# Odd mixer of a transformer kernel: products with V moved behind the next weight tile, ropes in two parts, output projection begun early

## The reference, cut to what matters

```python
DL_HEADS = 16; DL_HEAD_DIM = 64
DL_PAIRS = ((128, 1), (512, 4), (2048, 16))

def odd_mixer(x, w_in, w_out, cos, sin):
    B, S, D = x.shape
    q, k, v = jnp.split(x @ w_in, 3, axis=-1)
    ...
    q = partial_rope(heads(q), cos, sin) * (DL_HEAD_DIM ** -0.5)
    k = partial_rope(heads(k), cos, sin)
    v = heads(v)
    outs, lses = [], []
    for (w, d) in DL_PAIRS:
        o, lse = dilated_branch(q, k, v, d, w // d)
        ...
    wts = jax.nn.softmax(jnp.stack(lses, axis=0), axis=0)
    o = jnp.einsum('gbhs,gbhsd->bhsd', wts.astype(v.dtype), jnp.stack(outs, axis=0))
    return o.transpose(0, 2, 1, 3).reshape(B, S, D) @ w_out

mix = odd_mixer(x, od_w_in[j], od_w_out[j], cos, sin)
x = layer_norm(ALPHA * x + mix, ln1_g[l], ln1_b[l])
```

## Time and profile before

| | |
|---|---|
| median of 3 runs | 3791.18 us (3788.5 to 3801.71) |
| the profiled execution, its own time | 3791.59 us |
| its span | 3789.8 us |
| TensorE busy | 3436.3 us, 91% |
| VectorE busy | 2059.0 us, 54% |
| ScalarE busy | 1491.5 us, 39% |
| odd mixer, first attention step to the projection's start | 3052 to 3298 us |
| projection | 3298 to 3342 us |

### The profile page before, as it was taken

How to read it: one execution, slowest core, us unless ns; L and a number is a source line. 1 busy time by engine, 2 the same in 40 slices (tenths; PEclk the granted TensorE clock), 3 DMA queues, 4 the chain that set the end, 5 groups by cost and what they waited for, 6 DMA issues and landing times.

```text
span 3789.8 us, 59831 instructions
## 1 busy us (share of the span) xinstructions
PE 3436.3 (91%) x24660; PEld 2733.8 (72%) x24660; DVE 2059.0 (54%) x3388; ACT 1491.5 (39%) x2714; POOL 224.9 (6%) x455
## 2 busy tenths in 40 slices
PE   6888899999989958778899999789999989799999
PEld 4755788888866647676688887566888666568886
DVE  4377443334476747774544456655445655454446
ACT  5478342222246533334433334424333534343334
POOL 0011000000000014333100000000000000000000
PEclk8999999999999968999999999879999999899999
DMA  4122123321134677764222221111222211112221
GB/s 191 45 79 90 57 111 141 137 100 67 56 112 144 173 192 173 170 165 148 78 90 99 100 100 67 37 62 67 100 100 89 77 66 45 50 67 91 98 100 56
DMA packets 294414, 378.22 MB, mean 100 GB/s; under 512 B 240449, under 2 KB 243393, under 8 KB 259585
## 3 DMA queue, kind: packets, MB, share of 16 engines
q1 hardware_dynamic: 280912, 328.78, 27.0%
q10 hardware_dynamic: 13232, 45.61, 3.6%
HBM read 330.30 MB, written 44.06 MB: 99 GB/s over the span
## 4 chain that ended last, share of the span: by engine, by line
PE 79%; DVE 9%; ACT 6%; issue 3%; DMA 2%; POOL 0%; SPq 0%; ACTq 0%; DVEq 0%; POOLq 0%
PE ps L257 19%; PE ps L258 18%; PE ps L259 18%; PE ps L1368 1%; PE ps L1370 1%; PE ps L1369 1%; PE ps L339 1%; DVE wlo L249 1%; PE ps L803 1%; PE ps L789 1%; PE ps L2889 1%; PE ps L2213 1%; PE ps L2195 1%; PE ps L2223 1%; PE ps L3877 1%
## 5 line engine op out<-in xcount | busy, mean ns | idle before, releaser
L242 ACT ACTIVATE whi<-panel 128x512 fp32r<-128x512 f32 (+1 forms) x517 | 435.2, 842 | 585.7 <-PE ps L259 574.0
L249 DVE TENSOR_TENSOR wlo<-panel,whi 128x512 fp32r<-128x512 f32 (+1 forms) x517 | 495.8, 960 | 235.5 <-ACT whi L242 226.2
L257 PE MATMUL ps<-dh,whi 128*128 128x512 f32 (+1 forms) x1280 | 474.6, 371 | 0.0
L258 PE MATMUL ps<-dh,wlo 128*128 128x512 f32 (+1 forms) x1280 | 471.7, 369 | 0.0
L259 PE MATMUL ps<-dl,whi 128*128 128x512 f32 (+1 forms) x1280 | 471.4, 368 | 0.0
L257 PE MATMUL ps<-xh,whi 128*128 128x512 f32 x1088 | 443.2, 407 | 25.1 <-DVE xl L2930 19.2
L258 PE MATMUL ps<-xh,wlo 128*128 128x512 f32 x1088 | 429.2, 395 | 0.0
L259 PE MATMUL ps<-xl,whi 128*128 128x512 f32 x1088 | 428.8, 394 | 0.0
L257 PE MATMUL ps<-hh,whi 128*128 128x512 f32 (+1 forms) x960 | 352.8, 367 | 26.0 <-DVE hl L460 25.9
L258 PE MATMUL ps<-hh,wlo 128*128 128x512 f32 (+1 forms) x960 | 340.3, 354 | 0.0
L259 PE MATMUL ps<-hl,whi 128*128 128x512 f32 (+1 forms) x960 | 339.8, 354 | 0.0
(11 more groups left out here) (537 smaller groups left out, 5763.7 us busy)
## 6 DMA issues: line engine op xcount, KB each, us to landing
panel<-in_w SPq DMA_DIRECT2D x246, 1024.0 KB, 4.8
late<-s_fe ACTq DMA_DIRECT2D x16, 1024.0 KB, 5.7
late<-s_fe ACTq DMA_DIRECT2D x48, 256.0 KB, 3.9
s_fe<-x SPq DMA_DIRECT2D x24, 256.0 KB, 3.3
late<-s_fe ACTq DMA_DIRECT2D x8, 768.0 KB, 6.2
s_fe<-xx SPq DMA_DIRECT2D x16, 256.0 KB, 2.7
s_fe<-ctx SPq DMA_DIRECT2D x24, 128.0 KB, 2.9
s_ia<-panel SPq DMA_DIRECT2D x24, 128.0 KB, 4.0
```

The lines of the kernel that those rows point to most:

```text
L242: e.activation(unit(u)[0][:, 0:kc, :], w, ACT.Copy).then_inc(*w_hi.up(u))
L249: e.tensor_tensor(lo[:, 0:kc, :], w, hi[:, 0:kc, :].bitcast(F32), SUB).then_inc(*w_lo.up(u))
L257: e.matmul(out, hi[:, k, :], xh, start=k == 0, stop=False)
L258: e.matmul(out, lo[:, k, :], xh, start=False, stop=False)
```

## The change

1. `OSTEPS` has steps ("v", n): the products with V of unit n, with ScalarE's eviction of them, are taken out of attention step n+2 and stand behind the next "p" step (in the last units behind a part of the projection). What stays in the attention step is the transposes (`turned`). The transposes of a head wait for the scaled weights of that head alone.
2. The products alternate between an even and an odd head.
3. The last group's units go from four key blocks to one, so 12 is the longest and 15 the shortest (`LUNITS`).
4. Step ("a", 12) comes behind ("p", 22). Parts of the projection's first two tiles stand between the last units as steps ("w", (m, k0, k1)); they accumulate in banks 6 and 7. ScalarE's and VectorE's splits of the mixer's output stand in the steps "v" of units 10, 11 and 15 (`OPARTS`).
5. The rope of a tile is in two parts: the sine product stays in "r"; the cosine product and the sum go, if an attention step (other than a group's first) follows directly, between VectorE's evictions of the second and third scores.

The diff, cut to its core:

```diff
...
-    def pe_tile(e, u, out, x):
+    def pe_tile(e, u, out, x, k0=0, k1=None):
         kc = UNITS[u][1]
...
         e.wait_ge(*w_lo.at(u))
-        for k in range(kc):
+        for k in range(k0, kc if k1 is None else k1):
             xh, xl = x(k)
...
-        def __init__(self, u0, mm, ac, dv, src, segs, add, tail, then, ready=None):
-
-            self.ready = ready
+        def __init__(self, u0, mm, ac, dv, src, segs, add, tail, then, ready=None, begun=0, bank=lambda t: B[t % 6]):
+
+            self.ready, self.begun, self.bank = ready, begun, bank
             self.u0, self.mm, self.ac, self.dv, self.src, self.segs, self.add = u0, mm, ac, dv, src, segs, add
...
                     t = m * ns + s
-                    if t > 5:
+                    if t > 5 and not self.begun:
                         e.wait_ge(*self.dv.at("res", t - 6))
...
                         x = self.waited(e, s, x)
-                    pe_tile(e, self.u0 + m, B[t % 6][:, 0:sg[1]], x).then_inc(*self.mm.up(*self.key(m, s)))
+                    pe_tile(e, self.u0 + m, self.bank(t)[:, 0:sg[1]], x, 6 if m < self.begun else 0).then_inc(
+                        *self.mm.up(*self.key(m, s)))
+
+        def begin(self, e, m, k0, k1):
+            pe_tile(e, self.u0 + m, self.bank(m)[:, :], self.waited(e, 0, self.src(self.segs[0])), k0, k1)
...
                     e.wait_ge(*self.mm.at(*self.key(m, s)))
-                    self.add(e, m, sg, B[t % 6][:, 0:sg[1]]).then_inc(*self.dv.up("res", t))
+                    self.add(e, m, sg, self.bank(t)[:, 0:sg[1]]).then_inc(*self.dv.up("res", t))
             self.tail.tile_dve(e, 8 * ns - 1, self.dv.at("res", 8 * ns - 1))
...
     pj_odo = Proj(OU + 24, od_mm, od_ac, od_dv, lambda sg: hsrc(OXH, OXL, sg), [MAIN], alpha_add, ffn1.n1, (ffn1.f0,),
-                  lambda s, k: od_dv.at("lo", k))
-    LUNITS = [(g, qb) for g in range(4) for qb in range(4)]
+                  lambda s, k: od_dv.at("lo", k), 2, lambda t: B[(6, 7, 2, 3, 4, 5, 0, 1)[t]])
+    LUNITS = [(g, qb if g < 3 else 3 - qb) for g in range(4) for qb in range(4)]
     LBASE = [sum(LUNITS[x][1] + 1 for x in range(n)) for n in range(16)]
...
         _n, _t = 4 * _g, 6 * _g + 6
-        OSTEPS += [("a", _n), ("r", _t - 1), ("p", _t), ("p", _t + 1), ("r", _t), ("a", _n + 1), ("r", _t + 1), ("p", _t + 2),
-                   ("a", _n + 2), ("r", _t + 2), ("p", _t + 3), ("p", _t + 4), ("r", _t + 3), ("a", _n + 3), ("r", _t + 4),
-                   ("p", _t + 5)]
-    OSTEPS += [("a", 8), ("r", 17), ("p", 18), ("p", 19), ("r", 18), ("a", 9), ("r", 19), ("p", 20), ("a", 10), ("r", 20),
-               ("p", 21), ("a", 11), ("r", 21), ("a", 12), ("p", 22), ("p", 23), ("r", 22), ("a", 13), ("r", 23), ("a", 14),
-               ("a", 15), ("a", 16), ("a", 17)]
+        OSTEPS += [("a", _n), ("r", _t - 1), ("p", _t), ("v", _n - 2), ("p", _t + 1), ("r", _t), ("a", _n + 1), ("r", _t + 1),
+                   ("p", _t + 2), ("v", _n - 1), ("a", _n + 2), ("r", _t + 2), ("p", _t + 3), ("v", _n), ("p", _t + 4),
+                   ("r", _t + 3), ("a", _n + 3), ("r", _t + 4), ("p", _t + 5), ("v", _n + 1)]
+    OSTEPS += [("a", 8), ("r", 17), ("p", 18), ("v", 6), ("p", 19), ("r", 18), ("a", 9), ("r", 19), ("p", 20), ("v", 7),
+               ("a", 10), ("r", 20), ("p", 21), ("v", 8), ("a", 11), ("r", 21), ("p", 22), ("v", 9), ("a", 12), ("p", 23),
+               ("r", 22), ("v", 10), ("a", 13), ("r", 23), ("w", (0, 0, 4)), ("v", 11), ("a", 14), ("w", (1, 0, 4)), ("v", 12),
+               ("a", 15), ("v", 13), ("w", (0, 4, 6)), ("a", 16), ("w", (1, 4, 6)), ("v", 14), ("a", 17), ("v", 15)]
+    OSTEPS = [(kind, i) for kind, i in OSTEPS if kind != "v" or i >= 0]
     ROTS = [t for kind, t in OSTEPS if kind == "r"]
+    OPARTS = {10: (0, 1, 2, 3), 11: (4, 5), 15: (6, 7)}
...
             nk = qb * P + P
-            if qb == 0 and half == 0:
+            if n % 4 == 0 and half == 0:
                 for i in range(4):
...
-        def out(n):
-            g, qb = LUNITS[n]
-            S, Pt, o = D4[n % 3], DP[n % 2], B[4]
-            if qb == 0:
-                e.wait_ge(*od_dv.at("v", 6 * g + 4))
-                e.wait_ge(*od_dv.at("v", 6 * g + 5))
-            e.wait_ge(*dl_dv.at("prob", n, 3))
+        def turned(n):
+            qb, S = LUNITS[n][1], D4[n % 3]
             for b in range(qb + 1):
...
                 for i in range(4):
+                    if b == 0:
+                        e.wait_ge(*dl_dv.at("prob", n, i))
                     x = e.transpose(B[2 + t % 2][:, i * P:i * P + P], S[:, i, b * P:b * P + P], ID)
...
+
+        def values(n):
+            g, qb = LUNITS[n]
+            Pt, o = DP[n % 2], B[4]
+            if n % 4 == 0:
+                e.wait_ge(*od_dv.at("v", 6 * g + 4))
+                e.wait_ge(*od_dv.at("v", 6 * g + 5))
             if n > 0:
...
             e.wait_ge(*dl_ac.at("pt", LBASE[n] + qb))
-            for i in range(4):
-                rows, col = slice(64 * (i % 2), 64 * (i % 2) + 64), (i // 2) * P
+            for col in (0, P):
                 for b in range(qb + 1):
-                    x = e.matmul(o[rows, col:col + P], V8[g % 2][:, b, i * 64:i * 64 + 64], Pt[:, b, i * P:i * P + P],
-                                 start=b == 0, stop=b == qb)
+                    for h in range(2):
+                        i = col // 64 + h
+                        x = e.matmul(o[HALF[h], col:col + P], V8[g % 2][:, b, i * 64:i * 64 + 64],
+                                     Pt[:, b, i * P:i * P + P], start=b == 0, stop=b == qb)
             x.then_inc(*dl_mm.up("o", n))
...
                 turn(i)
+            elif kind == "v":
+                values(i)
+            elif kind == "w":
+                if i == (1, 0, 4):
+                    e.wait_ge(*od_dv.at("v", 23))
+                pj_odo.begin(e, *i)
             else:
...
                 if i > 1:
-                    out(i - 2)
+                    turned(i - 2)
                 if i < 16:
...
-        def out(n):
-            g, qb = LUNITS[n]
-            for b in range(qb + 1):
+        def turned(n):
+            for b in range(LUNITS[n][1] + 1):
                 t = LBASE[n] + b
...
+
+        def out(n):
+            g, qb = LUNITS[n]
             e.wait_ge(*dl_mm.at("o", n))
...
                 if i > 1:
-                    out(i - 2)
+                    turned(i - 2)
                 if i < 16:
                     soft(i)
-                if i == 14:
+            elif kind == "v":
+                out(i)
+                if i in OPARTS:
                     e.wait_ge(*od_mm.at("unit", OU + 23))
-                    e.wait_ge(*dl_ac.at("o", 11))
-                if i > 13:
-                    for k in ((0, 1), (2, 3), (4, 5), (6, 7))[i - 14]:
-                        if k == 6:
-                            e.wait_ge(*dl_ac.at("o", 15))
+                    for k in OPARTS[i]:
+                        e.wait_ge(*dl_ac.at("o", 2 * k + 3 - k % 2 * 2))
                         high(k)
...
                 return
-            a, b, d = OTQ[2 * (t % 2)][:, :], OTQ[2 * (t % 2) + 1][:, :], od_q(t)
+            b = OTQ[2 * (t % 2) + 1][:, :]
             if g > 1:
...
+
+        def rope(t):
+            a, b, d = OTQ[2 * (t % 2)][:, :], OTQ[2 * (t % 2) + 1][:, :], od_q(t)
+            if is_v(t):
+                return
+            e.wait_ge(*od_dv.at("sin", t))
             e.tensor_tensor(d, a, OCS[:, 0, :], MUL).then_inc(*od_dv.up("cos", t))
...
             for i in range(4):
+                if i == 2 and late:
+                    rope(late.pop())
                 e.wait_ge(*dl_mm.at("score", n, i))
...
-        for kind, i in OSTEPS:
+        late = []
+        for (kind, i), (then, n) in zip(OSTEPS, OSTEPS[1:] + [("", 0)]):
             if kind == "p":
...
                 turn(i)
-            else:
+                if then == "a" and n % 4:
+                    late.append(i)
+                else:
+                    rope(i)
+            elif kind == "a":
                 if i < 16:
...
                     soft(i - 1)
-                if i > 14:
-                    for k in ((0, 1), (2, 3), (4, 5))[i - 15]:
-                        low(k)
-        low(6)
-        low(7)
+            elif kind == "v" and i in OPARTS:
+                for k in OPARTS[i]:
+                    low(k)
         pj_odo.dve(e)
...
     o_out = sig("out_stored")
```

## The result

| | before | changed |
|---|---|---|
| median | 3792.36 us (4 runs, 3788.5 to 3801.71) | 3759.11 us (4 runs, 3754.59 to 3761.36) |
| ratio | | 0.9907, 95% interval 0.9886 to 0.9928 |
| profiled execution, its span | 3791.59, 3789.8 us | 3761.36, 3759.6 us |

The change saves 33 us, 0.9%; the forecast was 3755.5. In the profiled execution the span is 30.2 us shorter. From the first scores of step 0 to the end of the projection it is 30.9 shorter (289.0 before, 258.1 now); I call that the mixer stretch. What lies before it is 1.0 longer, what lies after it 0.3 shorter.

The account below looks back on a forecast made before the run. TensorE bounds the kernel, PE busy 91% of 3789.8 us. Gains of 9.7 (steady units), 5.4 (gap before unit 12) and 21 (last units and projection) sum to 36.1, so 3791.6 − 36.1 = 3755.5 us, range 3745 to 3771.

Parts of the forecast that it names:

- The steady units: Attention units up to 10, gains by position in a group less V between tiles: 9.7 us saved.
- The first position in a group: Units 4 and 8: V and step take 3.65 instead of 5.75 us, gain 2.1 each.
- V between two tiles: V of units 0, 2, 4, 6 costs full length and two switches: 0.65, 1.5, 0.65, 1.5, together −4.3 us.
- The gap before step 12: TensorE's 6.36 us wait for tile 21's rope gets tile 22 and V of 9 inside: gain 5.4 us.
- Units 12 to 15 and the projection: Last units through projection's end: less idle and low clock, gain 24.0 less 3 for a low-clock stretch, 21 us.
- The pairs' 3 us: V alternating two heads at 0.056 us per record saves 0.22 on 24 records, 0.54 on 32; 3 us in all.
- Pairs not overlapping: Rival: V's records stay 0.073 us apart in long units, 3 us lost, about 3759 us; chance 0.1.
- The low clock in the last units: Rival: gaps and small matmuls keep the clock low there, 9 us more, about 3764 us; chance 0.18.
- ScalarE's and VectorE's queues as the bound: Rival, last units: splits queue ahead of copies, idle 17 instead of 8.3 us, about 3764 us; chance 0.15.
- taken back later: Rival: stages after the mixer lose the gain to lower clock or panel waits, about 3785 us; chance 0.05.
- Slower: Rival: V and gaps between tiles bring the low clock into the steady part, 3811 us or more; chance 0.03.
- does what it says: Rival: the change doesn't, only the late rope could be void; 6 to 8 less gain, 3763 us; chance 0.04.

Follow-up runs that it names:

- second profile: The unaltered changed kernel run and profiled once more: ratio 0.9911 to the kernel before, mixer stretch 253.9 us.
- the kernel with the last units rearranged: Changed kernel with splits behind step 13's copies, V 11 ahead of tile 0's first part, tile 0's last blocks behind V 15, four blocks of tile 1 begun: ratio 0.9905.

## Why the prediction was right, by its steps

**The steady units (9.7).** In the first profile the part from step 0 to the end of tile 21 took 161.0 where 166.2 stood: 5.2 saved. In the second profile of the same kernel it was 157.1 less 0.6 for V of unit 8, which that window holds: 9.7, the number forecast. The two differ in no wait:

```profile
3053.80:3214.80 161.00, 150.03 (x759) 107.92 (x758) 92.46 (x171) 62.76 (x149) 0.00 (x0) 0.96 0.15 53
```

```profile
3048.80:3205.90 157.10, 145.77 (x767) 105.59 (x766) 92.45 (x171) 62.98 (x150) 0.00 (x0) 0.99 0.15 54
```

Idle is 11.0 and 11.3; busy time differs by 4.3 and the clock by 0.03. That the second profile met the number is luck. At the lower clock this part had 8.3 us of busy time before, 13.7 in the first changed profile and 3.2 in the second. With half of each taken off it went from 162.1 to 154.2 and 154.9, so the change itself saved 7.2 to 7.9. The step had no term for the clock, and two of its sizes were off.

The first position in a group gained 1.35, not 2.1. Step 4 before and now:

```profile
3114.91 1.09 PE L3892 MATMUL ps<-cst,s 128*128 128x128 f32 x8
3116.68 0.66 PE L3892 MATMUL ps<-cst,s 128*128 128x128 f32 x4 [0.67 <-ACT p L3950]
3118.11 1.77 PE L3901 MATMUL ps<-p,v 128*64 128x128 f32 x24 [0.78 <-ACT p L3950]
```

```profile
3114.89 1.09 PE L3913 MATMUL ps<-p,v 128*64 128x128 f32 x16
3115.92 0.49 PE L3884 MATMUL ps<-k,q 64*128 64x128 f32 x4
3116.34 1.09 PE L3896 MATMUL ps<-cst,s 128*128 128x128 f32 x8
3117.96 0.66 PE L3896 MATMUL ps<-cst,s 128*128 128x128 f32 x4 [0.53 <-ACT p L3967]
3118.68 0.68 PE L3884 MATMUL ps<-k,q 64*128 64x128 f32 x4
```

The forecast counted 1.8 for the transposes. That is the time from the first (3114.91) to the start of the last four (3116.68), and these take 0.66 more. So V and step now take 4.40, not 3.65. (Step 8 of the first profile, behind a tile at the lower clock, takes 3.80.)

V between two tiles cost 1.7 and 0.9 instead of 1.5 and 0.65: a change of kind costs about 0.2, not 0.1. The other positions came as worked out: step 5 with its turn 4.95 (forecast 4.95), step 6 with its V 4.83 where it took 4.73, step 2 no gain, step 7 5.9 for 7.2. A group's period at full clock is 58.6 (second profile; 60.1 in the first, with one dip in it), where it was 61.6 and 57.3 was forecast.

**The gap before step 12 (5.4).** 12.77 after tile 21 against the forecast's 12.6, with tile 22 done. Right, and shown from the other side by putting the step back.

**Units 12 to 15 and the projection (21).** 84.3 us, and 84.6 in the second profile, where the walk gave 80.7 and I added 3 for the clock. Each named wait was there: 1.5 and 0.76 in step 13, 0.78 before V 15, 2.01 for the last low part, 1.0 for unit 26, though the second profile doesn't have this last one. Idle time is 7.5 and 6.5, where the walk had 8.3 (the waits that it lists add up to 8.05). The lower clock cost 1.5 and 3.1 of the 3, and it began 45.7 and 45.5 us after the first scores of step 12, in the 41 to 48 where I expected it. The rest of the first profile is tiles, 50.2 where I had 49.0 (a part of twelve matmuls is 2.94 long, half a tile 2.72), and other work, 25.1 where I had 23.4. So the sum is off by under 1 because the misses offset each other.

**The reasons were less right than the sum.** I priced the parts one by one and added. At full clock that is nearly how it is: taken out of the changed kernel, V later costs about 10 us, the late rope 6, the place of step 12 4.5, the order 4.5, the pairs 3 and the early parts 2.5. That is 30 where the whole change is worth 23, so some parts are worth more beside the others than alone. The pairs' 3 us were right. What the forecast priced only in the last units is the clock. V later, the order and the pairs each save 5.3, 2.4 and 3.8 alone at full clock, and in each of these runs the lower clock took 5.0, 7.3 and 2.3 back; the ratios, 1.0000, 1.0012 and 1.0000, show no gain. In the whole change it went the other way: of the 30.9 us, 22.8 are idle time and 8.1 are the clock that came back with it (23.5 and 11.6 in the second profile). I hadn't walked the version without the early parts before predicting; it would have shown how little they add.

**Rivals.** Pairs not overlapping: shown wrong, by V's lengths in both directions. The Trainium skill (TensorE: Matmul & The Clock Gate, "Part 3") says that weight loads overlap running matmuls only where the row group differs. By that rule V of 32 records would have stayed at 2.5 us; the trace doesn't agree, it has 1.97. The low clock in the last units and ScalarE's and VectorE's queues as the bound: neither at the price given (idle 7.5, not 17; clock 0.98 from step 12 on), though the kernel with the last units rearranged, with its 1.98 us in step 14, shows the latter close by. Nothing was taken back later: 448.0 us followed the mixer stretch before, 447.7 after. Slower: no. The late rope does what it says, by the 0.60 above.

**Open.** What sets off a particular dip of the clock wasn't settled; the same program had 0.96 and 0.99 over the same part. So it isn't shown either that the parts taken alone must lose to the clock what they gain.

## What to carry to other kernels

A wait that stands at a queue's head may hide a second one behind it: before taking work out of a step, see what the work covers (here VectorE's eviction of scores) and shorten that in the same change. Walk the queues with every part in place, then once without each part: that also finds the part that buys little. Compare TensorE's busy and idle time of a stretch apart, since an equal program can differ by 3.5 us in busy time through the clock alone. Then take off half of the busy time at the lower clock: only that made parts of 2 to 5 us readable here.

## What the runs showed of the hardware that I had not expected

Removing waits can bring back more than the waits: without the late rope 6.4 us of idle time cost 11.7 us, and 6.0 of that is clock (9.6 of 15.9 against the second changed profile; two profiles of one program differ by 3.6 in this). Moving waits can cost though there are fewer: with the order alone idle time fell by 2.0 us and the stretch grew by 4.9, at a clock of 0.90 for 0.92. Two float32 products that alternate between the lower and upper 64 output partitions overlap although both use all 128 rows: 32 records in 1.97 us instead of 2.54, in pairs that start 7 ns apart. And a change between weight tiles and products with V has a price of about 0.2 us: V of 24 records between two tiles adds 1.7 us, 24 records of 0.056 are 1.3.
